# Hybrid encoder kernel: query projection of the expert router two heads ahead, in four pieces between expert tiles, and a reordered first chunk

## The chip, the cores and the metric

The kernel runs on one core of one Trainium2 chip. The metric is device time in microseconds (us): the median of three executions of the kernel before is 3581.2 us (3580.19 to 3581.97). One further execution was recorded by the profiler; it took 3575.37 us, of which the trace spans 3573.5 us.

## The reference, cut to what matters

The program is a trunk of two layers on 256 tokens of width 2048, all in float32. Layer 0 mixes tokens with a chunked mLSTM, layer 1 with grouped-query attention. Each is followed by a PEER channel mixer, which looks up experts by product keys:

```python
def peer(xn, wq, k1, k2, u, v):
    q = (xn @ wq).reshape(B, S, PEER_HEADS, 2, PEER_HALF)      # 8 heads, 2 sides of 128
    s1 = jnp.einsum('bshd,nd->bshn', q[..., 0, :], k1, ...)    # 128 keys a side
    s2 = jnp.einsum('bshd,nd->bshn', q[..., 1, :], k2, ...)
    t1, i1 = lax.top_k(s1, PEER_TOPK)                          # 16 of 128
    t2, i2 = lax.top_k(s2, PEER_TOPK)
    ...                                                        # 16 best of the 256 pairs
    gate = jax.nn.softmax(top_s, axis=-1)
    ...
    def block(args):                                           # 128 tokens at a time
        act = jax.nn.gelu(jnp.einsum('td,ted->te', x_blk, u[i_blk], ...))
        return jnp.einsum('te,ted->td', (g_blk * act).astype(v.dtype), v[i_blk])
```

Every token fetches 8 x 16 rows of `u` and as many of `v`, each of 2048 floats (8 KB).

## The kernel before, in words

**Stages.** In order of time: norm and input projection of the mLSTM (12 chunks of 512 columns), its scan and output projection (4 chunks), experts of layer 0, attention (6 and 4 chunks), experts of layer 1. The tokens lie in two blocks of 128 partitions.

**Projections.** A chunk of weights arrives in four quarters of 1 MB (rows of 2 KB), in ring slots 0 to 3. ScalarE (ACT) makes the high part of each quarter (L332), VectorE (DVE, chunk 0) or GpSimd (POOL, the others in this stage) the low part (L338), and TensorE (PE) multiplies three products of the parts (L770). A quarter's next load waits for `w_used`. The normed tokens are transposed by PE (L747) and split by ACT (L318) and DVE (L325).

**Expert stage.** It has 16 units a layer: 8 heads of token block 0, then 8 of block 1. A unit has 16 tiles; tile k is row k's expert of all 128 tokens. For each tile POOL gathers 1 MB of `u` into one of 4 ring slots (L450) and 1 MB of `v` into one of 8 (L459), in turn `u`, `v`, `u`, `v` on one in-order queue. A `u` gather waits until DVE has used its slot, a `v` gather until PE has. DVE makes the dot products of tile k (L1256). After each 4 tiles DVE prepares the gelu (L1263 to L1265), ACT does its tanh (L613), DVE ends it after the next tile's dot product (L1271, L1273), and ACT writes the four weights as diagonal matrices (L618). PE then adds 4 matmuls of 512 columns a tile to the result (L941). After tile 8's dot product DVE picks the next unit's experts (`topk`, from L1057 to L1117).

**Router.** A head's scores for both token blocks are made by `router`: PE multiplies the tokens (stationary) with 256 columns of query weights (L821, 32 matmuls of 256 columns, which the profile shows as 64 entries, since each float32 matmul is two), ACT copies the result (L594), PE transposes it (L829), ACT copies that (L597), PE multiplies with the keys (L836), ACT stores the scores (L599). Head h + 1 is done in unit h of block 0, on PE between tiles 3 and 4, on ACT ahead of the tanh of tiles 4 to 7. Head 0 is done before the first unit, in two halves by token block, its weights in ring slots of `v`. SyncE (SP) loads the 2 MB of query weights of head h when `rq_full` tells that head h - 1's projection is done (L394): two transfers of 1 MB in rows of 1 KB, into one pair of slots.

Every engine does its instructions in the order of the program; nothing is planned at run time.

Of the kernel before, what the change touches and what calls it, by code (L numbers as in the profile page):

```python
# [19 lines left out]
P = 128  # L20
# [66 lines left out]
def trunk_kernel(nc, consts, x, ln_mix, ln_ffn, m_w_in, m_gate_bias, m_head_norm, m_w_out,  # L87
# [11 lines left out]
    HEADS = wq.shape[2] // (2 * P)  # L99
# [8 lines left out]
    with ExitStack() as ctx:  # L108
# [86 lines left out]
        rq_full, rq_out, rt_full, rt_out, sc_full, sc_out = (sem(n) for n in ("rq_full", "rq_out", "rt_full", "rt_out", "sc_full", "sc_out"))  # L195
# [62 lines left out]
        q_nat, q_T, onehot = tile(2 * 2 * P), tile(2 * 2 * P), tile(512)  # L258
# [106 lines left out]
        def _(sp):  # L365
# [4 lines left out]
            sp.dma_start(w_gate[:, :].rearrange("p (k n) -> p k n", n=16),  # L370
                         m_w_in[0, :, 2 * NQK + 2 * NV:].rearrange("(k p) n -> p k n", p=P)).then_inc(wg_in, 16)
            sp.dma_start(bias[:, :], m_gate_bias[0].rearrange("t h -> (t h)").partition_broadcast(P)).then_inc(wg_in, 16)

            def load_chunks(w, first, n, column=0):

                with sp.Fori(0, n) as c:
# [6 lines left out]
            def load_queries(l):  # L383
# [6 lines left out]
                half = D // 2  # L390

                def load(h, slots=wq_slot, landed=wq_landed):
                    for i in range(2):
                        sp.dma_start(slots[i], wq[l, i * half:(i + 1) * half, bass.ds(h * (2 * P), 2 * P)]  # L394
                                     .rearrange("(k p) n -> p k n", p=P)).then_inc(landed[i], 16)
# [6 lines left out]
            load_chunks(m_w_in[0], *W_CH["m_in"])  # L402
# [91 lines left out]
        def _(act):  # L494
# [54 lines left out]
            load_gain(1)  # L549
            act.wait_ge(wg_in, 32)  # L550
            copy(w_gate_hi[:, :], w_gate[:, :]).then_inc(wg_hi, 1)
            project(mproj, 0, 2)
# [34 lines left out]
            def peer(l):  # L587

                def router(h, blocks=slice(0, NB)):
# [4 lines left out]
                    nc.scalar.copy(q_nat[:, lo * 2 * P:hi * 2 * P], mis[0][:, lo * 2 * P:hi * 2 * P]).then_inc(rq_out, 1)  # L594
                    act.wait_ge(rt_full, n + 1)
                    q_t = [t.rearrange("p (s t) -> p s t", s=2)[:, :, lo * P:hi * P] for t in (q_T[:, :], trb[0][:, :])]
                    nc.scalar.copy(*q_t).then_inc(rt_out, 1)  # L597
# [132 lines left out]
        def _(pe):  # L730
# [116 lines left out]
            for b in range(NB):  # L847
                norm(0, "n0", b)
# [637 lines left out]
```

## Time and profile before

| | |
|---|---|
| median of three executions | 3581.2 us |
| profiled execution | 3575.37 us |
| its span, first to last instruction | 3573.5 us |
| PE busy | 2921.2 us (82%) |
| DVE busy | 1814.9 us (51%) |
| POOL busy | 1687.3 us (47%) |
| ACT busy | 550.0 us (15%) |
| moved by DMA | 1228.67 MB, mean 344 GB/s |

### The profile page before, as it was taken

Reading aid. Unit: us, or ns where it says so; the run is one execution under the profiler, and the core shown is the slowest. Engines: PE = TensorE matmul, PEld = TensorE weight load, DVE = VectorE, ACT = ScalarE, POOL = GpSimd, SP = SyncE. Lnnn points to the kernel's source line nnn. Section 1 sums busy time; section 2 is a strip of 40 time slices with the busy share of each in tenths; the row PEclk is TensorE's granted clock in tenths of the full one; section 3 lists DMA queues with packets and bytes.
Section 4 is the critical chain, followed back from the end, with each engine's and each line's share of the span. In section 5 each row is a group of like instructions: output and inputs, shape, how many; then the busy total and the mean of one; then the engine's idle time right before and its main releaser. Section 6 shows DMA issues by size and latency. Waiting matters only on the chain.

```text
span 3573.5 us, 28551 instructions
## 1 busy us (share of the span) xinstructions
PE 2921.2 (82%) x8424; PEld 1619.7 (45%) x8424; DVE 1814.9 (51%) x3343; ACT 550.0 (15%) x1123; POOL 1687.3 (47%) x1137
## 2 busy tenths in 40 slices
PE   7999977888888877777779896788788877777877
PEld 6876743444444333333337784344444433333333
DVE  2021145555555556656555644555555555666564
ACT  3344210000000100000013431000000010000001
POOL 4767634444445455555531004444444445545553
PEclk9999989999999988889989998999999988898888
DMA  5544579999998999999985346999999899999998
GB/s 207 176 148 147 177 283 381 378 384 383 387 384 362 420 420 421 420 421 420 421 354 177 118 158 274 375 374 383 385 386 385 363 420 420 421 420 421 420 421 341
DMA packets 240794, 1228.67 MB, mean 344 GB/s; under 512 B 21088, under 2 KB 54624, under 8 KB 108512
## 3 DMA queue, kind: packets, MB, share of 16 engines
q0 software_dynamic: 147456, 1073.81, 73.1%
q1 hardware_dynamic: 92560, 148.67, 12.5%
q10 hardware_dynamic: 720, 5.44, 0.4%
q8 instruction: 34, 0.56, 0.1%
q14 instruction: 24, 0.20, 0.0%
HBM read 1225.74 MB, written 2.10 MB: 344 GB/s over the span
## 4 chain that ended last, share of the span: by engine, by line
PE 33%; DMA 30%; issue 17%; POOL 10%; DVE 7%; ACT 2%; POOLq 0%; DVEq 0%; ACTq 0%; SPq 0%
DMA ring_sb<-in_peer_u_dram,idx_cur 30%; PE bank L941 19%; PE bank L770 6%; PE bank L821 6%; POOL w_parts L338 6%; POOL ring_sb L459 3%; DVE ring_sb L1256 3%; POOL ring_sb L450 2%; ACT diag L618 1%; PE bank L836 0%; PE bank L1022 0%; PE bank L994 0%; DVE shared L1105 0%; DVE shared L1109 0%; DVE shared L1110 0%
## 5 line engine op out<-in xcount | busy, mean ns | idle before, releaser
L941 PE MATMUL bank<-ring_sb,diag 128*128 128x512 f32 x4096 | 1952.5, 639 | 527.3 <-ACT diag L618 527.3
L1256 DVE CUSTOM_DVE_ANT_0 ring_sb<-ring_sb,arena 128x2048 f32<-128x2048 f32 x512 | 1169.4, 2293 | 927.8 <-DMA ring_sb<-in_peer_u_dram,idx_cur 927.4
L941 PEld LDWEIGHTS bank<-ring_sb,diag 128*128 128x128 f32 x4096 | 832.2, 206 | 1638.7 <-issue 1445.0
L459 POOL DMA_INDIRECT ring_sb<-in_peer_v_dram,idx_cur x512 | 683.0, 1334 | 733.9 <-PE bank L941 566.1
L450 POOL DMA_INDIRECT ring_sb<-in_peer_u_dram,idx_cur x512 | 652.9, 1275 | 616.2 <-DVE shared L1256 451.5
L770 PE MATMUL bank<-w_parts,actT_hi 128*128 128x512 f32 x1664 | 523.2, 396 | 14.6 <-DVE actT_lo L325 6.5
L338 POOL TENSOR_TENSOR w_parts<-ring_sb,w_parts 128x2048 fp32r<-128x2048 f32 x62 | 287.3, 4638 | 157.2 <-ACT w_parts L332 157.2
L770 PEld LDWEIGHTS bank<-w_parts,actT_hi 128*128 128x128 f32 x1664 | 316.5, 191 | 84.1 <-DVE actT_lo L325 7.8
L770 PE MATMUL bank<-w_parts,actT_lo 128*128 128x512 f32 x832 | 327.7, 394 | 0.0
L613 ACT ACTIVATE shared<-shared 128x4 f32<-128x4 f32 (+1 forms) x140 | 28.8, 206 | 1514.1 <-DVE shared L1265 1514.1
L332 ACT CAST w_parts<-ring_sb 128x2048 fp32r<-128x2048 f32 x104 | 198.2, 1910 | 352.4 <-DMA ring_sb<-in_mlstm_w_in_dram 164.3
L618 ACT ACTIVATE diag<-const,shared 128x128 f32<-128x128 f32 x512 | 166.3, 390 | 388.4 <-DVE shared L1273 352.6
L821 PE MATMUL bank<-arena,actT_sb 128*128 128x256 f32 x896 | 195.7, 379 | 0.0
L821 PEld LDWEIGHTS bank<-arena,actT_sb 128*128 128x128 f32 x896 | 170.2, 190 | 29.1 <-issue 6.7
L770 PEld LDWEIGHTS bank<-w_parts,actT_lo 128*128 128x128 f32 x832 | 158.9, 191 | 33.7
L338 DVE TENSOR_TENSOR w_parts<-ring_sb,w_parts 128x2048 fp32r<-128x2048 f32 x42 | 95.9, 2290 | 98.3 <-ACT w_parts L332 98.3
L1271 DVE SCALAR_TENSOR_TENSOR shared<-shared 128x4 f32<-128x4 f32 (+1 forms) x140 | 22.4, 160 | 225.9 <-ACT shared L613 225.9
L429 POOL TENSOR_TENSOR small<-small,const 128x1 f32<-128x1 f32 x8 | 4.5, 565 | 174.2 <-DVE small L1042 174.2
L594 ACT COPY shared<-bank 128x512 f32<-128x512 f32 (+1 forms) x18 | 9.7, 538 | 437.7 <-PE bank L821 437.7
L747 PE MATMUL bank<-const,arena 128*128 128x128 f32 x160 | 30.4, 349 | 56.7 <-DVE arena L1045 38.2
L429 POOL TENSOR_TENSOR q_r<-q_ms,const 128x8 f32<-128x8 f32 x5 | 14.5, 2900 | 121.6 <-DVE q_ms L1345 121.6
L445 POOL COPY idx_cur<-idx_next 128x16 uint32<-128x16 uint32 x32 | 43.1, 1347 | 49.1 <-DVE x_sb L1130 25.0
(161 smaller groups left out, 1120.1 us busy)
## 6 DMA issues: line engine op xcount, KB each, us to landing
ring_sb<-in_mlstm_w_in_dram SPq DMA_DIRECT2D x48, 1024.0 KB, 5.1
arena<-in_peer_wq_dram SPq DMA_DIRECT2D x28, 1024.0 KB, 11.6
ring_sb<-in_attn_w_in_dram SPq DMA_DIRECT2D x24, 1024.0 KB, 5.0
ring_sb<-in_mlstm_w_out_dram SPq DMA_DIRECT2D x16, 1024.0 KB, 5.0
ring_sb<-in_attn_w_out_dram SPq DMA_DIRECT2D x16, 1024.0 KB, 5.0
ring_sb<-in_peer_u_dram,idx_cur POOLq DMA_INDIRECT x512, 15.3
ring_sb<-in_peer_v_dram,idx_cur POOLq DMA_INDIRECT x512, 14.0
ring_sb<-in_peer_wq_dram SPq DMA_DIRECT2D x4, 1024.0 KB, 8.9
```

The costliest lines, as they stand in the source:

```text
L332: nc.scalar.copy(w_hi_of[j], ring[j]).then_inc(w_hi, 1)
L338: ops.tensor_tensor(w_lo_of[j], ring[j], w_hi_of[j].bitcast(F32), ALU.subtract).then_inc(w_lo[j], 1)
L445: nc.gpsimd.tensor_copy(idx_cur[par][:, :], idx_next[:, :]).then_inc(idx_taken, 1)
L450: nc.gpsimd.indirect_dma_start(out=u_slot[k % NU], out_offset=None, in_=u_rows, in_offset=bass.IndirectOffsetOnAxis(ap=idx_cur[par][:, k:k ...
L459: nc.gpsimd.indirect_dma_start(out=v_slot[k % NVS], out_offset=None, in_=v_rows, in_offset=bass.IndirectOffsetOnAxis(ap=idx_cur[par][:, k: ...
L613: nc.scalar.activation(e_th[:, k0:k1], e_in[:, k0:k1], ACT.Tanh, scale=GELU_C).then_inc(tanh_out, 1)
L618: nc.scalar.activation(diag[k % 4][:, :], ident, ACT.Copy, scale=e_w[:, k:k + 1]).then_inc(diag_ready, 1)
L747: last = tp(trb[at % 2][:, i * P:(i + 1) * P], src[:, f * P:(f + 1) * P], ident)
L770: last = mm(acc[2 * par + b][:, :], xp, wp, start=(j == 0 and k == 0 and i == 0), stop=(j == 3 and k == QK - 1 and i == 2), skip_group_che ...
L821: last = mm(mis[0][:, b * 2 * P:(b + 1) * 2 * P], actT[:, k, b * P:(b + 1) * P], slots[k // 8][:, k % 8, :], start=(k == 0), stop=(k == KT ...
L941: last = mm(acc[n][:, :], diag[k % 4][:, :], v_slot[k % NVS][:, n * CH:(n + 1) * CH], start=False, stop=end and k == TOPK - 1, skip_group_ ...
L1256: v.tensor_tensor_reduce(u_slot[k % NU], u_slot[k % NU], xn[b], 1.0, 0.0, ALU.mult, ALU.add, dots[:, k:k + 1]).then_inc(u_used, 1)
```

## The change

Five things are changed.

1. Which operand of the query projection stays in PE: the weights (128 x 128 pieces) are stationary now and the tokens move. The result is the transposed query at once, so that PE's transposes (L829), ACT's first copy (L594) and the tile `q_nat` are gone.
2. The query weights lie in memory by head and by partition, so that a slot of 1 MB is 128 rows of 8 KB.
3. The projection of a head is cut in four parts (side of the head by half of the 2048 rows), which stand on PE ahead of tiles 2, 4, 6 and 8; the scores stand ahead of tile 10. On ACT the query copy comes after the diagonals of tiles 8 to 11 and the score copy ahead of the last tanh.
4. The router is two heads ahead: head 1 is done before unit 0, head h + 2 in unit h, and units 6 and 7 have none.
5. At the program's start the four loads of chunk 0 come ahead of those of the gate weights and bias, the splits of weights and tokens alternate on ACT and DVE, and PE starts chunk 0 after the transposes of token block 0.

```diff
+                        sp.dma_start(slots[i].rearrange("p k n -> p (k n)"),
+                                     rows[bass.ds(h * P + l * HEADS * P, P), i * SLOT:(i + 1) * SLOT]).then_inc(landed[i], 16)
...
-            load_chunks(m_w_in[0], *W_CH["m_in"])
+            for j in range(4):
+                sp.dma_start(ring[j].rearrange("p (k n) -> p k n", n=CH),
+                             m_w_in[0, j * CH:(j + 1) * CH, 0:CH].rearrange("(k p) n -> p k n", p=P)).then_inc(w_landed[j], 16)
+            sp.dma_start(w_gate[:, :] ...
+            load_chunks(m_w_in[0], *W_CH["m_in"], skip=1)
...
# ACT
-            hi_groups(act, copy, "n0", range(8))
-            hi_weights(act, 0, range(3))
+            hi_weights(act, 0, [0])
+            hi_groups(act, copy, "n0", range(0, 4))
+            hi_weights(act, 0, [1])
+            hi_groups(act, copy, "n0", range(4, 8))
+            hi_weights(act, 0, [2])
...
+                def router_query(h, blocks=slice(0, NB)):
+                    act.wait_ge(rq_full, n + 1)
+                    q_t = [t.rearrange("p (s t) -> p s t", s=2)[:, :, lo * P:hi * P] for t in (q_T[:, :], mis[0][:, :])]
+                    nc.scalar.copy(*q_t).then_inc(rq_out, 1)
+                def router_scores(h, blocks=slice(0, NB)):
                     act.wait_ge(sc_full, n + 1)
...
-                        if j == 1 and head is not None:
-                            router(head)
+                        if j == 3 and head is not None:
+                            router_scores(head)
+                        if j == 2 and more:
+                            gate_exp(gu + 1)
...
-                        if j == 1 and more:
-                            gate_exp(gu + 1)
+                        if j == 2 and head is not None:
+                            router_query(head)
...
+                router_query(1)
+                router_scores(1)
...
-                with act.Fori(0, HEADS - 1) as h:
-                    unit(h + base, True, head=h + 1)
+                with act.Fori(0, HEADS - 2) as h:
+                    unit(h + base, True, head=h + 2)
+                unit(base + HEADS - 2, True)
# PE
+            ROUTER_PARTS = [(side, half) for side in range(2) for half in range(2)]
+            def router(l, h, blocks=(0, 1), parts=ROUTER_PARTS):
+                for side, half in parts:
+                    if side == 0: ...                       # wait for the slot of this half
+                    for k in range(8 * half, 8 * half + 8):
+                        last = mm(mis[0][:, side * T + t0:side * T + t1], slots[half][:, k % 8, side * P:(side + 1) * P],
+                                  actT[:, k, t0:t1], start=(k == 0), stop=(k == KT - 1), skip_group_check=True)
...
-                        if k == 4 and head is not None:
-                            router(l, head)
+                        if k in (2, 4, 6, 8) and head is not None:
+                            router(l, head, parts=[ROUTER_PARTS[k // 2 - 1]])
+                        if k == 10 and head is not None:
+                            router_scores(l, head)
...
                 seed(0)
-                with pe.Fori(0, HEADS - 1) as h:
-                    unit(h + base, False, head=h + 1)
+                router_scores(l, 0, (1,))
+                router(l, 1)
+                router_scores(l, 1)
+                with pe.Fori(0, HEADS - 2) as h:
+                    unit(h + base, False, head=h + 2)
+                unit(base + HEADS - 2, False)
...
-            for b in range(NB):
-                norm(0, "n0", b)
-            project(0, 2)
+            norm(0, "n0", 0)
+            project(0, 2, second=lambda: norm(0, "n0", 1))
```

PE, unit 0 of the experts in block 0, before; the semaphores name what a row waits for (`v_landed`: a `v` tile, `diag_ready`: ACT's diagonals).

```order
L941 MATMUL bank<-ring_sb,diag 128x512 [waits v_landed3,diag_ready]
L941 MATMUL bank<-ring_sb,diag 128x512 x3
L818 ISA
L821 MATMUL bank<-arena,actT_sb 128x256 [waits wq_landed1,wq_landed0]
L821 MATMUL bank<-arena,actT_sb 128x256 x31
L825 REGISTER_ALU
L829 MATMUL bank<-const,shared 128x128 [waits rq_out]
L829 MATMUL bank<-const,shared 128x128 x3
L836 MATMUL bank<-keysT,shared 128x128 [waits rt_out]
L836 MATMUL bank<-keysT,shared 128x128 x3
L938 REGISTER_ALU
L941 MATMUL bank<-ring_sb,diag 128x512 [waits v_landed4,diag_ready]
```

The same engine and unit in the change, from tile 7 on (its slot is `v_landed7`) to tile 10; L840 is the projection, L852 the scores.

```order
L959 MATMUL bank<-ring_sb,diag 128x512 [waits v_landed7,diag_ready]
L959 MATMUL bank<-ring_sb,diag 128x512 x3
L840 MATMUL bank<-actT_sb,arena 128x256 x8
L956 REGISTER_ALU
L957 REGISTER_ALU [waits diag_ready]
L959 MATMUL bank<-ring_sb,diag 128x512 [waits v_landed0]
...
L959 MATMUL bank<-ring_sb,diag 128x512 [waits v_landed1,diag_ready]
L959 MATMUL bank<-ring_sb,diag 128x512 x3
L848 REGISTER_ALU
L852 MATMUL bank<-keysT,shared 128x128 [waits rq_out]
L852 MATMUL bank<-keysT,shared 128x128 x3
```

Where 32 projection matmuls, four transposes and four score matmuls stood in one piece with two waits for ACT, at most 8 projection matmuls stand between two tiles, and the wait for ACT's copy comes two tiles behind the last of them.

ACT in the same unit, before: the router's three copies stand ahead of the second tanh (L613).

```order
L594 COPY shared<-bank 128x512 [waits rq_full]
L597 COPY shared<-bank 128x512 [waits rt_full]
L599 ISA [waits sc_full]
L599 COPY arena<-bank 128x2x256
L612 REGISTER_ALU
L613 ACTIVATE shared<-shared 128x4 [waits tanh_in]
```

And in the change, behind the diagonals (L630) of tiles 8 to 11 and ahead of the fourth tanh (L625).

```order
L630 ACTIVATE diag<-const,shared 128x128 [waits v_used]
L600 REGISTER_ALU
L602 COPY shared<-bank 128x512 [waits rq_full]
L609 ISA [waits sc_full]
L609 COPY arena<-bank 128x2x256
L624 REGISTER_ALU
L625 ACTIVATE shared<-shared 128x4 [waits tanh_in]
```

What moved is the tanh that waits behind the router: it is the one of tiles 12 to 15 now, and one copy fewer stands ahead of it.

PE at the start of the expert stage, in the change, between the seed of the result (x_sb, const) and the first tile: head 1 is new here.

```order
L852 MATMUL bank<-keysT,shared 128x128 [waits rq_out]
L852 MATMUL bank<-keysT,shared 128x128
L840 MATMUL bank<-actT_sb,arena 128x256 [waits wq_landed0]
L840 MATMUL bank<-actT_sb,arena 128x256 x7
L840 MATMUL bank<-actT_sb,arena 128x256 [waits wq_landed1]
L840 MATMUL bank<-actT_sb,arena 128x256 x23
L852 MATMUL bank<-keysT,shared 128x128 [waits rq_out]
L852 MATMUL bank<-keysT,shared 128x128 x3
...
L957 ISA [waits diag_ready]
L959 MATMUL bank<-ring_sb,diag 128x512 [waits v_landed0]
```

Before, the first tile came right behind the seed.

## Rows read from the trace of the kernel before

**Rows 1.** The page's line of GB/s moved, in 40 equal slices of the span.
```profile
GB/s 207 176 148 147 177 283 381 378 384 383 387 384 362 420 420 421 420 421 420 421 354 177 118 158 274 375 374 383 385 386 385 363 420 420 421 420 421 420 421 341
```

**Rows 2.** Windows of units 0, 3, 6, 7, 10: length, busy of engines, clock, DMA share, GB/s.
```profile
476.07:569.92 93.85, 69.66 (x214) 41.75 (x215) 47.16 (x87) 10.80 (x27) 44.34 (x35) 0.85 0.92 363
...
756.78:849.16 92.38, 75.34 (x206) 38.96 (x205) 48.46 (x91) 7.99 (x25) 43.45 (x34) 0.93 0.96 386
...
1033.93:1126.13 92.20, 75.94 (x205) 39.36 (x205) 48.70 (x91) 8.08 (x25) 43.86 (x33) 0.91 0.89 364
1126.13:1201.62 75.49, 57.26 (x125) 24.38 (x124) 45.33 (x88) 6.45 (x22) 41.73 (x33) 0.91 1.01 415
...
1363.42:1443.24 79.82, 62.82 (x129) 26.75 (x128) 48.37 (x91) 6.34 (x22) 42.52 (x34) 0.86 1.01 420
```

**Rows 3.** PE in unit 5, in order of time: start, length, instructions, [idle before it].
```profile
975.69 15.71 PE L941 MATMUL bank<-ring_sb,diag 128*128 128x512 f32 x32 [9.99 <-ACT diag L618]
991.24 13.98 PE L821 MATMUL bank<-arena,actT_sb 128*128 128x256 f32 x64
1005.90 0.66 PE L829 MATMUL bank<-const,shared 128*128 128x128 f32 x4 [0.68 <-ACT shared L594]
1007.23 1.16 PE L836 MATMUL bank<-keysT,shared 128*128 128x128 f32 x8 [0.67 <-ACT shared L597]
```

**Rows 4.** DVE in unit 5: end of the gelu of tiles 4 to 7, next dot product.
```profile
1009.25 0.17 DVE L1271 SCALAR_TENSOR_TENSOR shared<-shared 128x4 f32<-128x4 f32 x1 [14.53 <-ACT shared L613]
...
1018.44 2.28 DVE L1256 CUSTOM_DVE_ANT_0 ring_sb<-ring_sb,arena 128x2048 f32<-128x2048 f32 x1
```

**Rows 5.** POOL in unit 5: the gathers around the router.
```profile
995.53 0.94 POOL L450 DMA_INDIRECT ring_sb<-in_peer_u_dram,idx_cur  x1 [2.38 <-DVE shared L1256]
1016.23 1.12 POOL L459 DMA_INDIRECT ring_sb<-in_peer_v_dram,idx_cur  x1 [19.76 <-PE bank L941]
1021.54 2.21 POOL L450 DMA_INDIRECT ring_sb<-in_peer_u_dram,idx_cur  x1 [4.19 <-DVE shared L1256]
```

**Rows 6.** DMA queues from 500 to 1120 us (two rows), 1130 to 1830 us (third): MB, share.
```profile
q0 software_dynamic: 30473, 221.86, 87.9%
q1 hardware_dynamic: 12768, 12.71, 6.3%
...
q0 software_dynamic: 40389, 294.09, 101.2%
```

**Rows 7.** PE and POOL in unit 11, which has no router; PE in unit 1 (last row).
```profile
1480.77 15.76 PE L941 MATMUL bank<-ring_sb,diag 128*128 128x512 f32 x32 [9.24 <-ACT diag L618]
...
1506.85 0.94 POOL L459 DMA_INDIRECT ring_sb<-in_peer_v_dram,idx_cur  x1 [5.30 <-PE bank L941]
...
580.60 14.00 PE L941 MATMUL bank<-ring_sb,diag 128*128 128x512 f32 x32 [1.90 <-ACT diag L618]
```

**Rows 8.** Start of the expert stage of layer 0: PE, ACT and POOL.
```profile
482.76 3.87 PE L747 MATMUL bank<-const,arena 128*128 128x128 f32 x16 [13.06 <-DVE arena L1045]
487.30 9.02 PE L821 MATMUL bank<-ring_sb,actT_sb 128*128 128x256 f32 x32 [0.68 <-ACT actT_sb L305]
...
498.23 3.60 PE L931 MATMUL bank<-x_sb,const 128*128 128x512 f32 x8
511.36 15.77 PE L941 MATMUL bank<-ring_sb,diag 128*128 128x512 f32 x32 [9.53 <-ACT diag L618]
...
477.29 1.17 POOL L450 DMA_INDIRECT ring_sb<-in_peer_u_dram,idx_cur  x1 [0.99 <-POOL idx_cur L445]
...
517.65 0.94 POOL L459 DMA_INDIRECT ring_sb<-in_peer_v_dram,idx_cur  x1 [5.46 <-PE bank L941]
```

**Rows 9.** Program start: SP's issues, ACT's first weight split, PE's first products.
```profile
11.57 59.26 SPq L380 DMA_DIRECT2D ring_sb<-in_mlstm_w_in_dram  x11
...
26.02 1.90 ACT L332 CAST w_parts<-ring_sb 128x2048 fp32r<-128x2048 f32 x1
...
30.40 1.19 PE L770 MATMUL bank<-w_parts,actT_hi 128*128 128x512 f32 x2 [4.89 <-DVE w_parts L338]
```

More of the change, by code:

```diff
@@ L369, in _, with load_chunks @@
             sp.dma_start(xb[1], x[0, P:2 * P, :]).then_inc(x_in[1], 16)
[L370 to L376, printed above, removed]
+            def load_chunks(w, first, n, column=0, skip=0):
+                with sp.Fori(skip, n) as c:
                     for j in range(4):
@@ L593, in router @@
                     act.wait_ge(rq_full, n + 1)
[L594 to L597, printed above, removed]
+                    q_t = [t.rearrange("p (s t) -> p s t", s=2)[:, :, lo * P:hi * P] for t in (q_T[:, :], mis[0][:, :])]
+                    nc.scalar.copy(*q_t).then_inc(rq_out, 1)
+                def router_scores(h, blocks=slice(0, NB)):
+                    n = h + (l * (HEADS + 1) + 1) if blocks != slice(0, 1) else l * (HEADS + 1)
+                    lo, hi = blocks.start, blocks.stop
                     act.wait_ge(sc_full, n + 1)
@@ L631, in peer @@
                 copy_groups(name, 0, norm_dst)
-                router(0, slice(0, 1))
+                router_query(0, slice(0, 1))
+                router_scores(0, slice(0, 1))
                 gate_exp(base)
@@ new lines, in router @@
+                t0, t1 = blocks[0] * P, (blocks[-1] + 1) * P
+                for side, half in parts:
+                    if side == 0:
+                        if first:
+                            pe.wait_ge(wq0_landed[half], 16 * (l + 1))
+                        else:
+                            pe.wait_ge(wq_landed[half], h * 16 + l * (HEADS - 1) * 16)
+                    for k in range(8 * half, 8 * half + 8):
+                        last = mm(mis[0][:, side * T + t0:side * T + t1], slots[half][:, k % 8, side * P:(side + 1) * P],
+                                  actT[:, k, t0:t1], start=(k == 0), stop=(k == KT - 1), skip_group_check=True)
@@ L833, in router, with router_scores @@
+                if parts[-1] == ROUTER_PARTS[-1]:
+                    last.then_inc(rq_full, 1)
+            def router_scores(l, h, blocks=(0, 1)):
+                n = h + (l * (HEADS + 1) + 1) if blocks != (0,) else l * (HEADS + 1)
+                pe.wait_ge(rq_out, n + 1)
                 for b in blocks:
@@ L1142, in _ @@
                 norm(0, b, 0)
-            lo_groups(dve, "n0", range(8))
-            lo_weights(dve, v, 0, range(4))
+            lo_weights(dve, v, 0, [0])
+            lo_groups(dve, "n0", range(0, 4))
+            lo_weights(dve, v, 0, [1])
+            lo_groups(dve, "n0", range(4, 8))
+            lo_weights(dve, v, 0, range(2, 4))
             dve.wait_ge(wg_hi, 1)
@@ L1477 @@
                 a = a.transpose(0, 2, 1)
+            if name == "peer_wq":
+                layers, d, n = a.shape
+                a = a.reshape(layers, d // P, P, n // (2 * P), 2 * P).transpose(0, 3, 2, 1, 4).reshape(layers, n // (2 * P), P, -1)
             a = _np.ascontiguousarray(a)
```

41 lines of the change are left out of this document (12 added, 29 removed).

## The prediction

> **What bounds the kernel now.** I read the page's line of GB/s first. In two stretches, one in each half, the rate is 420 to 421 GB/s, and just ahead of each lies one of about 375 to 387 [rows 1]. The stage is the same, the experts; the first eight units of a layer differ from the last eight by the router alone. Cut into units (from one copy of a unit's indices to the next), a unit without router takes 79.8 us at a DMA share of 1.01: the DMA engines are never idle and nothing else sets its length. A unit with router takes 92.2 to 93.9 us at a share of 0.89 to 0.96 [rows 2]. So block 0 is bound by DMA engines that run dry once a unit.
>
> Where they run dry shows in unit 5. PE's router lies in one piece between tiles 3 and 4: 13.98 us of projection, then 0.68, 0.66, 0.67 and 1.16 us for copies, transposes and scores [rows 3]. ACT's tanh of tiles 4 to 7 stands behind the router's copies, so DVE waits 14.53 us for it, and only then does its top-k, up to the next dot product at 1018.4 [rows 4]. POOL's queue is in order: its `v` gather waits 19.76 us for PE's slot, and the `u` gather behind it 4.19 us more for DVE. From 996.5 to 1021.5 one gather is issued [rows 5]. That is 25 us, in which 2.49 us a tile of 1 MB (79.8 / 32) would take ten; what was in flight covers some 16 to 19 us of it.
>
> **The sum, part by part.**
>
> *The split and the move (parts 3 and 4).* After the change no piece of PE work between two tiles is longer than 3.5 us (8 of 32 projection matmuls of the 13.98 us). Does PE keep up? At the higher clock a group of four tiles takes 14.00 us [rows 7]. Groups 0 to 3 of a unit then hold 14.0 + 3.5, 14.0 + 7.0, 14.0 + 3.5 + 1.2 and 14.0 us: 71.2 us together, against 84.8 us of DMA time worked out below. Only group 1 (21.0 us) is near its period of 21.2. ACT's tanh of tiles 12 to 15 now waits for the scores: PE has them some 14.5 us after the diagonals of tile 8 are asked for (2.9 us rest of group 1, part 3.5, two tiles 7.0, scores 1.2), ACT's copy ends 0.6 us later, and DVE asks for the tanh three dot products on, at about 15. It fits by a hair, and a late tanh of 1 or 2 us costs nothing while 10 us of transfers are in flight. The wait of POOL for a `v` slot at the head of a group, 5.30 us where there is no router [rows 7], becomes about 9 to 10; three pairs of tiles are in flight then. So I take the dry time as gone.
>
> A layer's block 0 is then its bytes: 8 units x 79.8 = 638.4 us of gathers, and six loads of query weights (heads 2 to 7; the count in this stage is six before too). At the gathers' rate a load of 2 MB is two of their tiles, 5.0 us, together 30. Before, 12.71 MB of loads in rows of 1 KB took 6.3% of 620 us, 3.07 us a MB, beside 2.41 us a MB for the gathers of block 1 [rows 6]: 6.4 us a load. To 668.4 us come 5 us for filling the queue (first issue at 477.3, and a gain vector of 1 MB beside it in layer 0) and 2 us for the start of unit 0, next. Sum 675.4. Before, the eight units took 725.5 us, from 476.07 to 1201.62 [rows 2]. That is 50 us less in layer 0. Layer 1's slices show the same two rates for as long [rows 1], so I take the same there: -100 us. As a cross-check, the share falls short of 1.01 by 0.05 to 0.12 in seven windows of 92 to 94 us, on the whole some 43 us; less 3 that remain, plus 6 x 1.4 for the cheaper loads, is 48.
>
> *Head 1 before unit 0.* On PE 14.0 us of projection, 0.7 for the copy, 1.2 of scores and some 1.5 to the diagonals follow the seed that ends at 501.8: the first tile comes at about 519 instead of 511.4, and the `v` gather that waits for it at about 525 instead of 517.65 [rows 8]. Issued by then are 9 `u` and 8 `v` tiles, 42 us of transfers from about 478.5 on, plus the gain load (2.5) and head 2's weights (5.0), which are now asked for at about 515: the engines have work to 528. I take 2 us for both blocks' remainders together; bounds 0 and 8 a layer (all of the delay).
>
> *Stationary weights (part 1).* For full heads 64 entries of 256 columns stay what they are. For head 0, in halves by token block, 32 entries of 256 columns become 64 of 128. The nearest row has 16 such entries in 3.87 us with waits between, and the bounds for one are 0.11 us (half of 0.218) and 0.22 us (width bringing nothing): 7.0 to 14 us instead of 7.2 to 9.0 [rows 8]. I take 0.13, 8.5 us. One transpose step and copy go (about 1.3 us). Net 0, bounds -1 and +6 at each of the two places where a layer's first indices wait for it.
>
> *Program start (part 5).* The weights are issued at 3 us instead of 11.57, ACT's split can start at about 16 instead of 26.02, and PE's first products at about 24.5 instead of 30.4 [rows 9]. But chunk 0 now contains block 1's transposes and two splits that ACT reaches late (the third after the eighth token group, about 35): PE stops for some 5 us in its middle and for a little more ahead of quarter 2. I get its end at about 52.5 where it was about 54. The later chunks are bound by PE at 5.45 us a quarter, with POOL's split at 5.5 beside it, so the shift stays: -2 us, bounds -6 and +5.
>
> Together: 3573.5 - 100 - 2 = 3471.5 span, 3473.4 as an execution (1.9 outside the span). The median of three lay 5.8 us above the profiled one, so 3479 us.
>
> **A rule against it.** The gathers in rows of 8 KB take 2.41 us a MB and the loads in rows of 1 KB 3.07 [rows 6]; so I let the new rows run at 2.41. The Trainium skill (DMA: Bandwidth & Descriptors, Specifications) puts the least size for full rate at 512 B, by which 1 KB rows are already wide enough and 8 KB rows bring nothing. By the row the layout is worth 1.4 us x 12 of the 100, by the rule none of it. The trace does not bear the rule out.
>
> **The rivals.**
>
> *A: a gap remains.* Group 1 has two parts on PE and falls together with the 9 us of top-k on DVE; the `v` slots of tiles 12 to 15 come free later than in block 1. If that still empties the queue for 3 us in each of 12 units, 36 us come back: 3515 us. For it: PE's group 1 fills its period. Against it: block 1 has the same top-k and shows share 1.01 [rows 2].
>
> *B: the loads get no cheaper,* because what they cost is not the row width but that SP's transfers mix with POOL's. 12 x 1.4 = 17 us: 3496 us. Against it are only the rates of rows 6. The skill's rule above would give this time as well.
>
> *C: PE becomes the bound, slower than before.* PE's 71.2 us a unit hold at 2.4 GHz. If pieces and waits leave its granted clock at 1.2 GHz for part of the work, a unit grows by as much; above 30% of the work at the low level (71.2 x 1.3 = 92.6) PE alone is slower than the unit before, and at half it is 107 us: 12 x 14.4 us more than before, about 3750. For it: the clock does fall in each wait for diagonals, and a burst of four tiles takes 15.7 us after one instead of 14.0 [rows 3, 7]. Against it: units with router (but for unit 0, whose start is idle) show a mean of 0.91 to 0.93 of the full clock, unit 10 without one 0.86 [rows 2]: more work on PE raised it.
>
> *D: the change does not do what it says,* since what empties the queue is the top-k after all: about 3581, within 0.2%. Against it, again, block 1.
>
> **Chances.** Forecast 0.76 (3465 to 3492), A 0.12, B 0.07, C 0.03, D 0.02. A difference below 0.2% (7 us) can't be told from none here. Faster 0.95, same 0.02, slower 0.03. The range takes in B and most of A: 3464 to 3512 us.
>
> **What would show it.** Router units at 84 to 86 us with a DMA share of 1.00 to 1.01 and 420 GB/s; units 6 and 7 near 80; no wait of DVE for the tanh above 3 us; POOL's longest wait for PE under 11 us; loads of query weights at 2.4 to 2.5 us a MB; the first PE tile of a layer some 7 us later after the first gather; PE's first product near 24.5 us. The forecast is wrong if the DMA share of router units stays under 0.98, or if PE's busy time in them passes 80 us.

## The result, and the profile after

The changed kernel takes 3446.8 us (median of 4 runs, 3443.9 to 3450.9) against 3580.7 of the kernel before: a ratio of 0.9634, with a 95% interval of 0.9610 to 0.9657. Forecast were 3479 us and a range down to 3464: the direction and the mechanism are right, the gain is 134 us and not 102, and the time lies below the range.

The profiled execution took 3443.88 us with a span of 3442.1, 131.4 less than before. Counted from one unit's index copy to the next, the difference lies here: up to the first unit 7.1 us (476.07 to 468.99); block 0 of layer 0 58.2 (725.5 to 667.3) and of layer 1 61.2 (725.1 to 663.9); all else (both blocks 1, the stage between the layers, the end) 4.9. Windows of units 0, 4, 5, 6 and 10, as in [rows 2]: start:end, length, busy time of PE, PEld, DVE, ACT, POOL, clock, DMA share, GB/s.

```profile
468.99:552.64 83.65, 72.38 (x285) 50.41 (x286) 45.47 (x86) 10.11 (x25) 43.29 (x35) 0.91 0.97 395
...
806.70:891.47 84.77, 71.92 (x200) 37.75 (x199) 48.08 (x91) 7.51 (x24) 39.85 (x34) 0.94 1.01 420
891.47:976.71 85.24, 72.21 (x202) 37.95 (x201) 48.11 (x91) 7.51 (x24) 39.48 (x34) 0.92 1.01 419
976.71:1056.52 79.81, 63.48 (x147) 28.32 (x146) 48.16 (x91) 7.62 (x24) 45.22 (x34) 0.92 1.01 420
...
1296.45:1376.24 79.79, 61.17 (x129) 25.99 (x128) 48.33 (x91) 6.33 (x22) 41.98 (x33) 0.89 1.01 421
```

From unit 1 on a router unit is now as full as one without a router: share 1.01, 420 GB/s, and it is longer by its loads alone. Unit 0, in which the queue fills, stays at 0.97. The gap of [rows 3 to 5] is gone. On PE (unit 4, in order of time; L959 x16 is two expert tiles, L840 a projection piece) no piece of the router is longer than 3.6 us:

```profile
849.21 9.17 PE L959 MATMUL bank<-ring_sb,diag 128*128 128x512 f32 x16 [10.70 <-ACT diag L630]
858.22 3.62 PE L840 MATMUL bank<-actT_sb,arena 128*128 128x256 f32 x16
861.67 7.03 PE L959 MATMUL bank<-ring_sb,diag 128*128 128x512 f32 x16
868.54 3.62 PE L840 MATMUL bank<-actT_sb,arena 128*128 128x256 f32 x16
```

From 849 us on PE has no gap for 50 us; its spare time is the 10.70 us ahead of the first tile. Both facts matter below. DVE, which waited 14.53 us for the tanh [rows 4], waits 0.27, since ACT copies the scores 7 us before it needs them (last tiles of unit 3; the second row's idle time is ACT's wait for DVE):

```profile
815.62 0.59 ACT L609 COPY arena<-bank 128x512 f32 x1 [7.27 <-PE bank L852]
...
823.34 0.21 ACT L625 ACTIVATE shared<-shared 128x4 f32<-128x4 f32 x1 [7.13 <-DVE shared L1290]
823.58 0.17 DVE L1296 SCALAR_TENSOR_TENSOR shared<-shared 128x4 f32<-128x4 f32 x1 [0.27 <-ACT shared L625]
```

POOL's waits for PE in block 0 (552 to 1136 us: total, times, longest), where [rows 5] show one of 19.76:

```profile
POOL ring_sb L462 <- PE bank L959: 113.1, 37, 6.6
```

The DMA queues from 490 to 1050 us, as in [rows 6] (MB, share of 560 us). The loads in q1 take 2.42 us a MB (before 3.07), the gathers in q0 2.41 (before 2.46):

```profile
q0 software_dynamic: 30414, 221.49, 95.3%
q1 hardware_dynamic: 2016, 12.71, 5.5%
```

The start of the expert stage, as in [rows 8]: head 0 in 64 narrower products, head 1 behind it, and the first expert tile at 511.12, which is 42.1 us after the first index copy (before 35.3). Head 2's weights come 1.40 us late for the first piece. The last row of the second fence is PE's first product, 7.4 us earlier than in [rows 9].

```profile
480.23 9.54 PE L840 MATMUL bank<-actT_sb,ring_sb 128*128 128x128 f32 x64 [0.67 <-ACT actT_sb L305]
...
493.49 13.98 PE L840 MATMUL bank<-actT_sb,arena 128*128 128x256 f32 x64
511.12 7.13 PE L959 MATMUL bank<-ring_sb,diag 128*128 128x512 f32 x16 [1.83 <-ACT diag L630]
519.65 0.70 PE L840 MATMUL bank<-actT_sb,arena 128*128 128x256 f32 x2 [1.40 <-DMA arena<-in_peer_wq_dram]
```

```profile
19.57 1.97 PE L764 MATMUL bank<-const,arena 128*128 128x128 f32 x8 [6.06 <-DVE actT_lo L325]
22.98 1.19 PE L787 MATMUL bank<-w_parts,actT_hi 128*128 128x512 f32 x2 [1.45 <-DVE actT_lo L325]
```

### The profile page after: what moved, and what is told of

It reads as the page before. It is cut to its first block, busy times and chain, and to the rows that moved or that the text cites. A ratio compares the mean times of both kernels' runs of the same rounds, so it can differ in the third digit from the quotient of the medians.

```text
span 3442.1 us, 28533 instructions
## 1 busy us (share of the span) xinstructions
PE 2879.7 (84%) x8488; PEld 1609.9 (47%) x8488; DVE 1814.7 (53%) x3343; ACT 542.6 (16%) x1105; POOL 1643.0 (48%) x1137
## 4 chain that ended last, share of the span: by engine, by line
DMA 37%; PE 33%; issue 14%; POOL 10%; DVE 5%; ACT 1%; POOLq 0%; DVEq 0%; ACTq 0%; SPq 0%
DMA ring_sb<-in_peer_u_dram,idx_cur 36%; PE bank L959 20%; PE bank L787 6%; POOL w_parts L338 6%; PE bank L840 5%; POOL ring_sb L462 2%; DVE ring_sb L1281 2%; POOL ring_sb L453 1%; POOL idx_cur L448 1%; ACT diag L630 0%; PE bank L764 0%; PE bank L1044 0%; PE bank L1016 0%; DMA arena<-in_peer_wq_dram 0%; PE bank L1035 0%
## 5 line engine op out<-in xcount | busy, mean ns | idle before, releaser
L959 PE MATMUL bank<-ring_sb,diag 128*128 128x512 f32 x4096 | 1935.9, 633 | 457.7 <-ACT diag L630 457.7
L959 PEld LDWEIGHTS bank<-ring_sb,diag 128*128 128x128 f32 x4096 | 824.4, 204 | 1530.9 <-issue 1322.7
L462 POOL DMA_INDIRECT ring_sb<-in_peer_v_dram,idx_cur x512 | 672.6, 1314 | 635.1 <-PE bank L959 466.5
L453 POOL DMA_INDIRECT ring_sb<-in_peer_u_dram,idx_cur x512 | 616.2, 1203 | 634.8 <-DVE shared L1281 472.1
L787 PE MATMUL bank<-w_parts,actT_hi 128*128 128x512 f32 x1664 | 521.0, 395 | 12.6 <-DVE actT_lo L325 9.4
L625 ACT ACTIVATE shared<-shared 128x4 f32<-128x4 f32 (+1 forms) x140 | 28.8, 206 | 1607.0 <-DVE shared L1290 1607.0
L630 ACT ACTIVATE diag<-const,shared 128x128 f32<-128x128 f32 x512 | 167.0, 391 | 461.4 <-DVE shared L1298 420.2
L840 PE MATMUL bank<-actT_sb,arena 128*128 128x256 f32 x896 | 201.7, 379 | 1.4 <-DMA arena<-in_peer_wq_dram 1.4
L840 PEld LDWEIGHTS bank<-actT_sb,arena 128*128 128x128 f32 x896 | 170.0, 190 | 45.3 <-issue 22.5
L448 POOL COPY idx_cur<-idx_next 128x16 uint32<-128x16 uint32 x32 | 45.7, 1427 | 47.8 <-DVE x_sb L1152 24.3
L764 PEld LDWEIGHTS bank<-const,arena 128*128 128x128 f32 x160 | 22.6, 171 | 64.6 <-DVE arena L1067 27.6
L305 DVE COPY actT_sb<-bank 128x512 f32<-128x512 f32 x10 | 6.9, 692 | 85.8 <-PE bank L925 78.0
## 6 DMA issues: line engine op xcount, KB each, us to landing
arena<-in_peer_wq_dram SPq DMA_DIRECT2D x28, 1024.0 KB, 12.7
ring_sb<-in_peer_u_dram,idx_cur POOLq DMA_INDIRECT x512, 15.3
```

What stands on the lines that cost most here:

```text
L448: nc.gpsimd.tensor_copy(idx_cur[par][:, :], idx_next[:, :]).then_inc(idx_taken, 1)
L453: nc.gpsimd.indirect_dma_start(out=u_slot[k % NU], out_offset=None, in_=u_rows, in_offset=bass.IndirectOffsetOnAxis(ap=idx_cur[par][:, k:k ...
L462: nc.gpsimd.indirect_dma_start(out=v_slot[k % NVS], out_offset=None, in_=v_rows, in_offset=bass.IndirectOffsetOnAxis(ap=idx_cur[par][:, k: ...
L625: nc.scalar.activation(e_th[:, k0:k1], e_in[:, k0:k1], ACT.Tanh, scale=GELU_C).then_inc(tanh_out, 1)
L630: nc.scalar.activation(diag[k % 4][:, :], ident, ACT.Copy, scale=e_w[:, k:k + 1]).then_inc(diag_ready, 1)
L764: last = tp(trb[at % 2][:, i * P:(i + 1) * P], src[:, f * P:(f + 1) * P], ident)
```

## The experiments

In each group the kernel before ran beside them on the same chip (medians 3577.0, 3574.3, 3574.2 and 3571.7 us), so the ratios to it compare best. Its median differs by up to 9 us between the groups (3580.7 beside the changed kernel), so a difference in us to the changed kernel's 3446.8 is loose by some us wherever the profiled times of block 0 don't bear it out. "Block 0" is the time of its eight units in layer 0 and in layer 1: 725.5 and 725.1 us before, 667.3 and 663.9 after.

### The memory layout undone

```
- rows[bass.ds(h*P + l*HEADS*P, P), i*SLOT:(i+1)*SLOT]          # 8 KB rows
+ wq[l, i*half:(i+1)*half, bass.ds(h*2*P, 2*P)]                 # 1 KB rows
```

> The changed kernel with the query weights in their old place in memory, so that a load of 1 MB is 1024 rows of 1 KB again; all else as changed. Theory (rows of 1 KB cost their own longer packet times, 1.4 us a load, and slow the gathers beside them by about 10 us a layer): the router units are still bound by DMA, so all of it shows: 2 x (8.4 + 10) = 37 us, about 3484 us, with gathers at 2.45 to 2.46 us a MB in block 0. Rival 1 (only the loads' own packet times): 2 x 8.4 = 17 us, about 3464 us, gathers at 2.41. Rival 2 (the row width is worth nothing): 3447 us.

Measured 3485.3 us, ratio 0.9740 (0.9718 to 0.9762), 38.6 us above the changed kernel: the total that was expected, but not where it was expected. A router unit in the steady state takes 85.9 us instead of 84.8 at a share of 1.02: the rate itself costs 1.1 us. That is the loads' own packet time (490 to 1050 us: 2.95 us a MB against 2.42, for 2.1 MB a unit); the gathers beside them went from 2.41 only to 2.43, not to the 2.45 that the theory needed. Unit 0 takes 101.5 us instead of 83.6, and in layer 1 98.3 instead of 84.0; these two make most of it. There PE waits 15.5 us for head 2's weights in both layers (first fence, layer 0), and the DMA engines run half empty behind it (windows, columns as above):

```profile
533.29 6.40 PE L840 MATMUL bank<-actT_sb,arena 128*128 128x256 f32 x16 [15.52 <-DMA arena<-in_peer_wq_dram]
```

```profile
520.00:530.00 10.00, 0.00 (x0) 0.00 (x0) 8.61 (x36) 0.69 (x2) 0.94 (x1) 0.58 1.03 404
530.00:540.00 10.00, 6.71 (x18) 5.25 (x19) 1.94 (x4) 0.00 (x0) 0.00 (x0) 0.56 0.45 167
540.00:550.00 10.00, 10.00 (x33) 6.00 (x32) 2.65 (x5) 1.10 (x4) 4.22 (x4) 1.00 0.43 153
```

Why so late shows in the time from issue to landing of a 1 MB load (490 to 1050 us; 1 KB rows, then the changed kernel):

```profile
arena<-in_peer_wq_dram SPq DMA_DIRECT2D x12, 1024.0 KB, 45.7
```

```profile
arena<-in_peer_wq_dram SPq DMA_DIRECT2D x12, 1024.0 KB, 12.7
```

### The memory layout alone, on the kernel before

The same edit the other way round, on the kernel before.

> The kernel before with the 8 KB rows alone. Theory (the units with router are bound by the wait of POOL, ACT and DVE on the router; a load is asked for when the queue runs dry and lies in the dry time): the units stay near 92 us and only their DMA share falls; 0 to -10 us against the kernel before, 3571 to 3581. Rival (dry time and cost of the rows simply add up): -37 us, about 3544.

Measured 3576.7 us, ratio 0.9999 (0.9989 to 1.0008). Block 0 takes 729.3 and 725.2 us, no less than before. The theory holds: while the stall sets a unit's length, faster loads only lengthen the dry time. The layout is worth nothing before the move and 39 us after it; the parts of this change don't add. The gathers from 500 to 1120 us still take 2.46 us a MB, as with 1 KB rows [rows 6]:

```profile
q0 software_dynamic: 30329, 220.80, 87.6%
```

### The operand swap alone, on the kernel before

```
- mm(mis0[b], actT[:, k, b], wq[:, k, :])                 # + 4 transposes, + 1 copy
+ mm(mis0[side], wq[:, k, side], actT[:, k, both blocks])  # query comes out transposed
```

> The kernel before with one thing changed: the query weights are the stationary operand of the projection, so that the query comes out transposed and the four transposes and one ScalarE copy of each head go. Placement (whole router before tile 4, one head ahead) and memory layout are as before. Theory: while DMA runs dry in each router unit, the stall is what sets a unit's length, so each of the 14 router units gets shorter by what goes from the stall: 0.70 us of transposes, one copy of 0.6 us and its hand-over, some 1.3 to 1.9 us, 18 to 27 us in all: 3550 to 3560 us, units at 91 to 92 us. Rival: 128-column products cost the same as 256-column ones where the weight load bounds them, or the stall is caught by the next unit's gathers: 3577 us, no change. A second rival: the whole gain of the change (3447 us) comes from it; excluded if over 3500 us.

Measured 3559.0 us, ratio 0.9959 (0.9943 to 0.9974). Block 0 takes 717.9 and 716.4 us, so 16.3 us are gone in 14 router units, 1.2 a unit: the 0.66 us of transposes and the 0.68 us of waiting for the copy ahead of them [rows 3]. What is taken out of the stall is taken off the unit, if a little less than was expected.

### The projection in one piece

```
- if k in (2, 4, 6, 8): router(l, head, parts=[ROUTER_PARTS[k // 2 - 1]])
+ if k == 4: router(l, head)              # the scores stay before tile 10
```

> The changed kernel with the projection in one piece ahead of tile 4 on PE (scores still ahead of tile 10, ACT's order as changed, two heads ahead). Theory (it is mainly the wait of ACT's tanh and with it of DVE that emptied the queue; PE's 14 us alone also hold POOL's v gathers back, some 16 us of transfers being in flight): a small gap comes back, 1 to 4 us in each of 12 units, 3460 to 3495 us. Rival 1 (PE's piece is the whole of it): units of 90 us or more, above 3510. Rival 2 (it is ACT and DVE alone): 3447.

Measured 3453.0 us, ratio 0.9657 (0.9636 to 0.9677): 6 us above the changed kernel, and below the 3460 us that the theory gave at least. The interval overlaps that of the changed kernel; block 0 takes 669.6 and 670.2 us, 2.3 and 6.3 more. Its router units take 83 to 89 us at a share of 1.01, but for unit 0 (0.97, 0.96) and the last one of each layer (0.98, 0.99). One block of 13.98 us stands on PE, POOL waits up to 13.7 us for a slot, and the queue stays full but in that last unit, since DVE goes on (it waits at most 0.3 us for the tanh):

```profile
865.33 13.98 PE L840 MATMUL bank<-actT_sb,arena 128*128 128x256 f32 x64
```

### Two heads ahead, but the whole router in the old place

```
- PE: parts before tiles 2, 4, 6, 8, scores before 10; ACT: query copy after the diagonals of 8 to 11
+ PE: projection and scores before tile 4;             ACT: both copies before the tanh of 4 to 7
```

> The changed kernel with the whole router in one piece ahead of tile 4, scores included, and both of ACT's copies ahead of the tanh of tiles 4 to 7, as before; two heads ahead, 8 KB rows and stationary weights kept. Theory (splitting and moving is the effect, being two heads ahead only allows it): DVE waits 12 to 14 us for the tanh again, units of 88 to 91 us, 12 x 3 to 6 us more: 3485 to 3520 us. Rival (being ahead is enough, since nothing waits for these scores): 3447 us.

Measured 3539.8 us, ratio 0.9901 (0.9884 to 0.9917), 93 us above the changed kernel and more than any theory gave. Block 0 takes 713.0 and 709.8 us, only 12.5 and 15.3 less than before; 7.6 and 8.7 of them are the operand swap's (above). The long waits of [rows 4] and [rows 5] are back, DVE's for the tanh first, POOL's for the slot and for PE behind it:

```profile
816.55 0.17 DVE L1294 SCALAR_TENSOR_TENSOR shared<-shared 128x4 f32<-128x4 f32 x1 [13.82 <-ACT shared L626]
821.99 0.93 POOL L462 DMA_INDIRECT ring_sb<-in_peer_v_dram,idx_cur  x1 [17.22 <-PE bank L957]
828.87 2.19 POOL L453 DMA_INDIRECT ring_sb<-in_peer_u_dram,idx_cur  x1 [5.94 <-PE bank L957]
```

Against the run ahead of it, 86.8 us faster, this differs in where the scores and ACT's two copies stand. So the stall was mainly ACT's: its copies waited for the router's products while DVE needed the tanh queued behind them. On PE the scores moved too; no run takes the two apart, but the scores are 1.16 us of products and 0.68 us of waiting, some 22 us in 12 units if all of it showed. Computing two heads ahead brings little by itself: block 0 is 4.9 and 6.6 us shorter than with the operand swap alone (717.9 and 716.4). It is what allows the copies to come so late.

### The program start undone

```
- load_chunks(..., skip=1); hi_weights(0,[0]); hi_groups(0..3); hi_weights(0,[1]); ...
+ load_chunks(...);         hi_groups(0..7); hi_weights(0,[0..2]); ...
```

> The changed kernel with the old program start: gate weights loaded first, then four loads of weight chunk 0, all activation splits before the first weight split, both normalisations before the first product. What is left of the change is the expert stages'. Theory: the new start brings 2.2 us at the evacuation of chunk 0, and the other 4 us by which the first unit of layer 0 starts earlier come from the weight chunks behind it and are nobody's but the start's while the stream of weights bounds them; so the first unit starts 2 to 6 us later than 468.99 and the kernel takes 3449 to 3453 us. Rival 1: the 7 us are all the start's (3453.8 us, first unit at 476). Rival 2: the time up to the first unit is bounded by the stream of weights and the start is hidden: first unit at 469 to 470, 3447 us; the 7 us would then belong to the new memory layout and the router of head 0.

Measured 3452.9 us (5 runs), ratio 0.9661 (0.9647 to 0.9674); span 3448.1, 6.0 above the changed kernel's. The first unit starts at 472.29, 3.3 us later; block 0 takes 667.3 and 663.9, to the tenth what it took. So the expert stages gain nothing from the start. The 6 us are about what these runs can tell (the two intervals overlap). How much of the 7.1 us belongs to the start stays open within a few us: over the fourteen profiles the first unit starts between 472.3 and 478.3 us with the old start and between 467.7 and 476.7 with the new one (medians 474.4 and 469.6).

### Head 2's pieces later, with 1 KB rows

```
- unit 0 of each layer: pieces before tiles 2, 4, 6, 8
+ unit 0 of each layer: two before tile 7, two before tile 8   (other units unchanged)
```

> The changed kernel with the query weights in the old layout (1 KB rows), as in the run that took 3485.3 us, but with head 2's pieces in unit 0 of each layer's block 0 moved back from before tiles 2, 4, 6, 8 to before tile 7 (two) and tile 8 (two); the other router units are unchanged. In the run before, TensorE waited 15.5 us in unit 0 for head 2's weights, which took 37.6 us from issue to landing in 1 KB rows beside the gathers (12.7 us in 8 KB rows), and the DMA share fell to 0.44 for 20 us. Theory: that wait is where most of the 38.6 us come from (17.9 us in unit 0 of layer 0, 14.3 us in that of layer 1), and it is the place of the first piece that makes it: unit 0 comes back to 84 to 86 us and the kernel takes 3451 to 3458 us. Rival: the loads of 1 KB rows cost their time at the start of the stage however late they are used: 3480 to 3487 us.

Measured 3471.8 us, ratio 0.9717 (0.9702 to 0.9732): 13.5 us back instead of 27 to 34, between the theory and its rival. In layer 1 it is as expected: no wait of PE for weights is left, unit 0 takes 79.3 us (98.3), and block 0 670.4 us, which is the changed kernel's and 1.1 us for each of six loads. In layer 0 unit 0 takes 100.2, for the loads are later still: the second one lands 50 us after its issue (509.0 to 559.0), with gathers beside it all the time (share 1.00 or more up to 560 us). The wait has moved with the piece:

```profile
538.13 3.72 PE L840 MATMUL bank<-actT_sb,arena 128*128 128x256 f32 x16 [0.54 <-DMA arena<-in_peer_wq_dram]
558.95 6.47 PE L840 MATMUL bank<-actT_sb,arena 128*128 128x256 f32 x16 [17.10 <-DMA arena<-in_peer_wq_dram]
```

So the late load is the cause of the wait. What makes it so late here is not shown: in layer 1 both loads had landed when PE asked for them, 29 us after their issue, beside gathers as well. One thing that differs is a gain vector of 1 MB that is loaded at the same time in layer 0 only.

### 2 KB rows

```
+ rows = wq ... "(j p n) -> j p n", n=512      # a head's 2 MB as 8 blocks of 128 rows of 2 KB
```

> The changed kernel with the query weights in 2 KB rows: in DRAM each head's 2 MB are eight blocks of 128 rows of 2 KB, and a load of 1 MB reads four of them. The loads of head 2 are issued at 507.6 us of layer 0 and TensorE asks for them some 12 us later; with 8 KB rows it waited 1.4 us, with 1 KB rows 15.5 us. Theory: beside a full gather queue a load advances by packets (a packet of it, then one of the gathers' 8 KB), so its time from issue to landing goes with its number of packets: median 11 us in 8 KB rows, 46 us in 1 KB rows in the steady router units, so 11 + (46 - 11) x (32 - 8) / (64 - 8) = 26 us in 2 KB rows (32 packets on each of 16 DMA engines); TensorE's wait in unit 0 becomes 1.4 + 24/56 x 14.1 = 7 to 8 us, some of it hidden; the kernel takes 3452 to 3464 us. Rival 1: what counts is the efficiency of a row, which is bad at 1 KB and good from 2 KB on: 3447 to 3450 us and landing at 11 to 13 us. Rival 2: a row that is not 8 KB long costs as much as one of 1 KB: 3485 us.

Measured 3461.6 us, ratio 0.9681 (0.9658 to 0.9705). PE waits 9.6 us in unit 0 of layer 0 (7 to 8 were expected), a steady unit takes 85.3 us, and a load lands after 27.7 us, where 26 was worked out from the number of packets:

```profile
535.48 5.98 PE L840 MATMUL bank<-actT_sb,arena 128*128 128x256 f32 x16 [9.61 <-DMA arena<-in_peer_wq_dram]
```

```profile
arena<-in_peer_wq_dram SPq DMA_DIRECT2D x12, 1024.0 KB, 27.7
```

12.7, 27.7 and 45.7 us for 1 MB as 8, 32 and 64 packets on each of 16 DMA engines: beside a full gather queue a load's latency was some 8 us and 0.6 us more for each packet.

### More work on TensorE, in four places

PE is busy 72 us of 84.8 in a router unit. How much more does it bear? First all four pieces of each head doubled, +14 us:

```
+ if len(parts) == 1:                       # between expert tiles
+     mm(trb[0], wq[:, k, side], actT[:, k])   # the same product once more, into a bank nobody reads
```

> The changed kernel in which each projection piece's eight products of the router are done twice when they stand between expert tiles (the second into a bank that nobody reads): 32 products of 0.22 us more, +14 us of TensorE work in each of the 12 router units, from 70 to 75 us to 84 to 89 us against a DMA period of 84.8 us. Theory (DMA bounds the router units and TensorE has 10 to 14 us to spare in each): the unit grows only by what passes 84.8 us, to 86 to 90 us, the kernel to 3447 + 12 x 1..5 = 3460 to 3510 us, with the DMA share falling below 1.00 for the first time. Rival 1: TensorE is on the path already (through what waits for its single pieces), so all 14 us show in each unit: 3447 + 12 x 14 = 3615 us. Rival 2: 3447 us, nothing, if the gaps between tiles are wider than the busy time says.

Measured 3529.2 us, ratio 0.9875 (0.9860 to 0.9890); from unit 1 on router units of 89 to 92 us at a share of 0.94 to 0.98 and a clock of 0.96 to 0.98. Of 14 us, some 6 show, more than the theory's 1 to 5 and less than half of what rival 1 gave. Then two pieces, +7 us, those before tiles 2 and 4 (`and side == 0`):

> The changed kernel with the eight products of the first two of a head's four projection pieces done twice between expert tiles (the second into a bank that nobody reads): +7 us of TensorE work in each of the 12 router units; doubling all four (+14 us) added 6.2 us to each router unit (91.0 against 84.8) and 82 us to the kernel. Theory: TensorE has 14 - 6.2 = 7.8 us to spare in a router unit, so 7 us more are hidden: 3447 to 3455 us, units 84.8 us at share 1.00 or 1.01. Rival: its spare time is no threshold; what is added shows in proportion, 44% of it, since each longer piece delays the next expert tile: +3.1 us a unit, 3484 us.

Measured 3494.4 us, ratio 0.9776 (0.9758 to 0.9794); steady units of 88.6 us. The threshold of 7.8 us falls, and the rival is nearer (3.8 us a unit, 54% of what was added, where it gave 3.1). But the loss has a place: in a window of 7.4 us behind the doubled pieces the DMA share drops to 0.79, in the window after that it is 0.96, in all others of the unit 0.99 or more:

```profile
903.18:910.58 7.40, 7.40 (x27) 4.83 (x26) 3.07 (x8) 0.90 (x3) 4.25 (x4) 1.00 0.79 290
```

The next run puts the same 7 us ahead of the unit's first tile:

```
+ if k == 0: 16 products of 128x256 into the same bank, before the wait for the first diagonal
```

> The changed kernel with 16 products of 128x256 more in each of the 12 router units (into a bank that nobody reads), the same +7 us of TensorE work as in the run that doubled two projection pieces, but put before the unit's first expert tile, where TensorE waits 10.7 us for the first ScalarE diagonal (849.21 us in unit 4 of layer 0). Doubling two pieces before tiles 2 and 4 cost 3.8 us a router unit and 47.6 us in all, though TensorE is busy only 72 of 84.8 us: there the pieces and tiles follow one another without a gap for 50 us and the DMA share falls to 0.79 behind them. Theory (the spare time stands in one place, ahead of the first tile): the 7 us are hidden there, units 84.8 us at share 1.00 to 1.01, 3446 to 3453 us. Rival (added TensorE work costs 54% of itself wherever it stands, by the total of busy time at a lowered clock): 3494 us, units 88.6 us.

Measured 3447.0 us, ratio 0.9648 (0.9632 to 0.9664); block 0 takes 666.8 and 665.1 us. All 7 us are hidden: PE's wait of 10.70 us has shrunk to 0.98, and the clock of units 1 to 5 has risen from 0.92 to 0.94 to 0.96 to 1.00.

```profile
839.89 7.07 PE L954 MATMUL bank<-actT_sb,keysT 128*128 128x256 f32 x32
847.94 7.13 PE L963 MATMUL bank<-ring_sb,diag 128*128 128x512 f32 x16 [0.98 <-ACT diag L630]
```

And the last one doubles the pieces before tiles 6 and 8 (`and side == 1`):

> The changed kernel with the other two pieces doubled, those before tiles 6 and 8: +7 us in each router unit at the end of the stretch in which TensorE has no gap. Theory (what counts is that the stretch from the unit's first tile to its scores gets 7 us longer before TensorE catches up): as with the first two pieces doubled, 3480 to 3500 us, units 87.5 to 89 us. Rival (a delay counts only from the tile on at which it is put; later tiles have more slack, since TensorE's wait before the next unit's first tile follows soon): clearly less, 3447 to 3470 us.

Measured 3460.0 us, ratio 0.9690 (0.9673 to 0.9706); block 0 takes 674.2 and 668.5, against 692.7 and 685.2 with the first two pieces doubled. The rival holds. The two blocks grow by 11.5 us in all where the first two pieces made it 46.7. The same 7 us cost 47.6, 13 and 0 us by their place. That fits a delay that, early in the stretch without gaps, holds back every `v` slot from there on, and near its end only the few ahead of PE's next wait; which slots it held back was not followed in the traces. Nor do the places add: all four pieces doubled cost 82 us, the two halves 61.

## Why the prediction was right in kind and wrong in size

**The move (parts 3 and 4): right.** The dry time went from some 43 us a layer to 3, tanh and POOL's waits came under their bounds, units came to 84.8 and 79.8, PE's busy time to 72 (71.2 forecast). Of the two halves of the move it is the order on ACT that counts (87 us, PE's scores with it, against 6 for the pieces). ACT's tanh does not fit "by a hair": the scores are copied 7.1 us before it is asked for. The prediction named ACT's tanh as the first link but then asked mostly whether PE keeps up.

**The block 0 term: the step that failed.** It set 675.4 us after, 668.4 for bytes and 7 on top, against a measured 725.5 before. Measured are 667.3 and 663.9, so 8.1 and 11.5 us too much. The single units came as charged, 84.8 and 79.8 us; the window of eight did not. The sum charged it with all its bytes (268.4 MB of gathers and 12.6 of loads, 281.0). But a unit's index copy comes while gathers of the unit before are in flight: length times GB/s over the eight windows gives 278.2 MB after, and 277.4 before (layer 1: 277.1 and 276.6). The measured 725.5 had that credit in it, my 675.4 did not: 2.8 MB at 420 GB/s are 6.7 us, in layer 1 3.9 MB and 9.3 us. 278.2 MB take 662 us, and 5 us of filling the queue make up the 667 (unit 0 moves 395 GB/s for 83.65 us, which is 5.0 us short of 420). The 2 us for head 1 were not needed: its first tile came 6.8 us later, as worked out, and the queue stayed full. The cross-check (48) missed in the same direction: it took 1.4 us for each cheaper load, 8.4 us, while the eight units' length less their dry time fell by some 19 us (725.5 - 42.7 = 683 to 664), because the gathers also went from 2.46 to 2.41 us a MB. That is not the layout's doing: with 8 KB rows on the kernel before they still took 2.46. They got faster where the dry time went; why is open.

**The layout: too small, and in the wrong place.** The forecast gave it 1.4 us x 12 = 17 us, all of it in the rate. Undone it costs 38.6 us, so 17 was too little; the total that came right is that of the expectation of 37 us, written with the result known. The rate makes some 13 of it (1.1 a unit) and head 2's late landing most of the rest. The trace of before could not show this: there the queue runs dry once a unit, and 1 KB loads landed in a median of 10.8 us (700 to 1000 us). Rival B is thus false. The Trainium skill (DMA: Bandwidth & Descriptors, Specifications) puts the least size for full rate at 512 B; for this load beside these gathers the measurement decides against it, with 2.95 us a MB in 1 KB rows against 2.42 in 8 KB rows.

**The operand swap: within its bounds.** Head 0's 64 narrow products took 9.54 us for 9.02 [rows 8] (forecast 8.5) at a clock of 0.76 over 480 to 490 us. At the full clock, for block 0, they take 7.41 us, 0.116 apiece, where 32 of 256 columns took 7.17 before, so half the columns is nearly half the time; the transposes and the copy come off on top.

```profile
451.29 7.41 PE L840 MATMUL bank<-actT_sb,ring_sb 128*128 128x128 f32 x64 [0.68 <-ACT actT_sb L305]
```

**The program start: too small.** -2 was forecast for the first unit; -7.1 was seen, -2.2 at the end of chunk 0's evacuation (55.65 to 53.49), and 3.3 go when the start alone is undone. The rest is within the scatter from run to run (467.7 to 476.7 us for the first unit), so the -7.1 is in part luck of the profiled run; the bounds of -6 and +5 had not been made for it.

**Rivals A and D: false.** No gap came back, and the top-k alone empties nothing.

**Rival C: still false, but nearer than thought.** No unit became longer by the clock. Yet a group "near its period" was the right worry: 7 us more ahead of tiles 2 and 4 cost 48 us.

Together: the two blocks 19, the start 5, and 5 us in block 1, between the layers and at the end, where nothing was forecast, are the 29.4 us by which the span's -131.4 passes the forecast -102. Another 2.7 us of the 32 by which the median was missed lie in the step from the profiled execution to it, 5.6 us forecast and 2.9 measured.

## What to carry to other kernels

Where an in-order queue stalls, move the waiting instruction, not the work it waits for: here the place of ACT's two copies, with the scores on TensorE, decided 87 us, cutting TensorE's projection into pieces 6. Judge an engine's spare time by where its gaps stand, not by busy against span; seven more us a unit cost anything from 0 to 48 in all by their place. And compare a window worked out from bytes with one measured only after giving both the same bytes in flight.

## What was new of the hardware

- A load of 1 MB beside a saturated gather queue landed after 12.7, 27.7 and 45.7 us in rows of 8, 2 and 1 KB (up to 50 us from issue), while the units' rate changed by 0, 0.6 and 1.3% (84.8, 85.3, 85.9 us). Short rows cost latency first and the units' rate little.
- More TensorE work raised its granted clock: 0.92 to 0.94 in the router units of the changed kernel, 0.96 to 0.98 with 7 us in place of its wait. What it did before the clock fell was to wait: a window of 7 us wholly within the wait of 10.70 shows 0.58, between the two levels, and the two tiles behind it took 9.17 instead of 7.03 us.

```profile
842.00:849.00 7.00, 0.00 (x0) 0.00 (x0) 4.33 (x9) 0.53 (x3) 1.88 (x2) 0.58 1.01 418
```
